# A routed mixture of experts in one core's kernel: another way to the top four, two wide places for four, and token selection turned round

## The chip, the cores and the metric

The kernel runs on one core of one Trainium2 chip. The metric is device time in microseconds for one execution; the median of three runs stands for the kernel.

## The reference

Three transformer blocks are applied to 256 tokens of width 1024, in fp32. The change lies in the first block's mixture of experts (32 experts, top 4, inner width 1024):

```python
logits = h @ w_router + b_router
top_v, top_i = lax.top_k(logits, 4)
gates = softmax(top_v)
# for each expert e, for the tokens xb that chose it:
u = xb @ w_mlp1[e] + b_mlp1[e]                      # 1024 -> 2048
x_glu = minimum(u[..., ::2], 7.0)
x_lin = clip(u[..., 1::2], -7.0, 7.0)
a = x_glu * sigmoid(1.702 * x_glu) * (x_lin + 1)
y = a @ w_mlp2[e] + b_mlp2[e]                       # 1024 -> 1024
# out[token] += gate * y
```

256 tokens and 4 choices make 1024 assignments, 32 an expert on average. The weights of an expert are 12 MiB, those of all 384 MiB.

## The kernel before

The program is written out by hand for five engines: a function `X_pe`, `X_act`, `X_dve` or `X_sp` holds what TensorE, ScalarE, VectorE or the loading queue (SyncE) does in stage X, in program order. Engines meet over counters: `then_inc(*k.DVE("perm"))` counts up and marks, `wait_ge(*k.dve("perm"))` waits. The eight PSUM banks are handed out by `k.bank` in rotation, and the next user of a bank waits until it has been read out. "Place" is the word for a position p = 0..31 in the order in which experts are worked on; "group" is a set of up to 64 or 128 slots for tokens in it.

**Router** (`route_pe`, `route_act`, `route_dve`). x lies with its 1024 features in eight chunks of 128 partitions (`x[:, c, :]`, 256 tokens wide). 16 matmuls (L1592) make the logits, tokens on partitions, 32 columns. `to_tok_pe` (L714) transposes x to token rows, `htok`. VectorE finds the four largest of 32 by counting for every logit how many stand above it: comparisons of all pairs, 1024 elements a partition, ties to the lower index (L1647 to L1660), and a mask of those with fewer than four above (L1663). Matmuls with a triangle of ones (L1598 to L1604) count each token's position within its expert and the experts' totals. From these VectorE makes `posm` (position or -1), the matrix `perm` that sorts experts by their totals (L1687), the gates, and on place 0 the selection matrix `P` (tokens x slots, a one where a token takes a slot).

**Order of the places.** Place 0 is always expert 0, so its weights can be loaded before the router is done. The other 31 experts are sorted by how many tokens chose them, and `RANKS` says which rank comes to which place. The places in `WIDE` get the largest ones and two groups (128 slots); all others have one group of `CAP = 64` slots. So there are 32 + len(WIDE) groups, and `OF[p]` lists those of place p. If any expert has more tokens than its place has slots, `count` is positive and `overflow_*` runs all experts again on a slow path.

**Experts** (`experts_pe`, from L1881). For each place p, TensorE goes through 8 up steps, c = 0..7, one for each chunk of `w_mlp1` (`up_pe`, L1781): for each group four matmuls with 64 stationary columns of `xg` (the selected tokens, features on partitions) and 512 moving columns of weights, in two column tiles (h = 0, 1) that run side by side. Between the steps stand other pieces: after c = 1 the transposes of the previous place's activation (`turn_a_pe`, L1828), after c = 3 the scatter of the place before that (L1868), after c = 5 the selection of the next place's tokens (`select_x_pe`, L1744) and the transposes of its gated selection matrix (`select_g_pe`, L1752). Then come the bias (L1792) and the previous place's 4 down steps (L1851). `select_x_pe` holds 16 matmuls a group:

```python
for d in range(KC):
    for b in range(2):
        m = e.matmul(bank[:, d * CAP:(d + 1) * CAP], t["htok"][:, b, d * 128:(d + 1) * 128], t[f"P{n % 3}"][:, b, :], start=b == 0, stop=b == 1)
```

**Weights** (`experts_sp`, L1959). Each load is 1 MiB and goes to one of `NEXP = 9` slots. Load m waits until load m - 9 has been used. Loads 0 to 7 (place 0's up) go out before the router is done; load 8 waits for `idx`, the sorted list of experts. A place has 8 up loads and 4 down loads, the latter behind the next place's up loads.

Of the kernel before, what the change touches and what calls it, by code (L numbers as in the profile page):

```python
# [16 lines left out]
KC = 8  # L17
# [5 lines left out]
WIDE = (0, 8, 16, 24)  # L23
# [8 lines left out]

RANKS = [NE - 1 if p == 0 else WIDE.index(p) - 1 if p in WIDE else p - 1 + sum(1 for w in WIDE[1:] if w > p) for p in range(NE)]

EARLY = ("tri", "swa1", "iota", "ids", "idcol", "keyrow", "keycol", "ranks", "r64", "r128", "r256", "b32", "pick2")


def const_arrays():  # L40
# [9 lines left out]
    c["pick2"] = ((i % 32 == 0) & (j < 64) | (i % 32 == 16) & (j >= 64)).astype(f32)  # L50
    c["tri"] = (i < j).astype(f32)
# [54 lines left out]
class Mute:  # L106
# [7 lines left out]
    copy_predicated = memset = dma_start = bn_stats = bn_aggr = If = nothing  # L114
# [1470 lines left out]
def route_pe(k, e):  # L1585
    t = k.t
    e.wait_ge(*k.act("pre2", "out", 3))
    e.wait_ge(*k.dve("pre2", "out", 7))
    bank = k.bank(e, "logits")
    for b in range(2):  # L1590
        for c in range(KC):
            m = e.matmul(bank[:, b * NE:(b + 1) * NE], t["x"][:, c, b * 128:(b + 1) * 128], t["wr"][:, c, :], start=c == 0, stop=c == KC - 1)  # L1592
# [16 lines left out]
    e.wait_ge(*k.dve("perm"))  # L1609
    perm = t["perm"][0:NE, :]  # L1610
    e.matmul(k.bank(e, "idx")[0:1, 0:NE], k.cc("idcol")[0:NE, :], perm).then_inc(*k.MM("idx"))
    bank = k.bank(e, "gT")
    e.wait_ge(*k.dve("gates"))
    for b in range(2):
        e.transpose(bank[0:NE, b * 128:(b + 1) * 128], t["gates"][:, b, :], k.cc("ident"))
        m = e.transpose(bank[0:NE, 256 + b * 128:256 + (b + 1) * 128], t["posm"][:, b, :], k.cc("ident"))
    m.then_inc(*k.MM("gT"))
    bank = k.bank(e, "perm")
    e.wait_ge(*k.act("gT"))
    for i in range(4):  # L1620
# [22 lines left out]
def route_dve(k, e):  # L1643
    t = k.t
    L, mask, gates, st = t["L"], t["mask2"][:, :, 0:NE], t["gates"], t["st"]
    ids = k.cc("ids")
    e.tensor_tensor(t["etri"], over(ids, NE), along(ids, NE), ALU.is_lt).then_inc(*k.DVE())  # L1647
# [3 lines left out]
    for b in range(2):  # L1651
        other, own = L[:, b:b + 1, :].to_broadcast([128, NE, NE]), along(L[:, b, :], NE)
        e.tensor_tensor(t["cmp0"], other, own, ALU.is_equal).then_inc(*k.DVE())
        e.wait_ge(*k.dve())
        e.tensor_tensor(t["cmp0"], t["cmp0"], t["etri"], MUL).then_inc(*k.DVE())
        e.tensor_tensor(t["cmp1"], other, own, ALU.is_gt).then_inc(*k.DVE())
        e.wait_ge(*k.dve())
        e.tensor_tensor(t["cmp0"], t["cmp0"], t["cmp1"], ADD).then_inc(*k.DVE())
        e.wait_ge(*k.dve())
        e.tensor_reduce(t["above"][:, b, :], t["cmp0"], AX.X, ADD).then_inc(*k.DVE())  # L1660
        e.wait_ge(*k.dve())
    for i in range(2):
        e.tensor_scalar(t["mask2"][:, :, i * NE:(i + 1) * NE], t["above"], 3.5, None, ALU.is_lt).then_inc(*(k.DVE("mask") if i else k.DVE()))  # L1663
# [2073 lines left out]
```

## Time and profile before

| | |
|---|---|
| median of 3 runs | 2960.89 us (2958.17 to 2964.32) |
| profiled execution, its own time | 2964.16 us |
| its span | 2962.3 us |
| mean granted TensorE clock | 0.953 |
| TensorE busy | 2793.4 us, 94% |
| VectorE, ScalarE busy | 47%, 31% |
| bytes moved | 713.75 MB, of them 384 loads of 1 MiB of expert weights |

The span runs from the first to the last instruction. Three stretches follow one another without overlap on TensorE: what lies before the router (0 to 235 us), router and experts (235 to 1311 us), and the two other blocks (to 2962 us).

### The profile page before, as it was taken

What the parts mean: (1) busy time and instruction counts of PE and PEld (TensorE: products, weight loads), DVE (VectorE), ACT (ScalarE), POOL (GpSimd) and SP (SyncE); (2) the same over time, 40 slices, a digit from 0 to 9 for tenths busy, and PEclk for the clock granted to TensorE, in tenths of its full rate; (3) what the DMA queues carried; (4) which work ended last, traced back from release to release, by engine and by line L of the source; (5) the groups of instructions that cost most, each with busy time, mean ns of one, the idle gap of its engine ahead of it and who ended that gap; (6) DMA issues with size and microseconds to landing.
All of it is one profiled execution on the core that took longest, in us unless ns stands there. A gap on an engine that the chain in (4) does not pass through costs nothing. (4 is left out here: it accounts for less than half of the span.)

```text
span 2962.3 us, 41639 instructions
## 1 busy us (share of the span) xinstructions
PE 2793.4 (94%) x17530; PEld 2006.9 (68%) x17530; DVE 1394.8 (47%) x1995; ACT 925.6 (31%) x1220; POOL 223.5 (8%) x160
## 2 busy tenths in 40 slices
PE   7887999999999999977899989999999999999998
PEld 5655344443443433426879979989889989898897
DVE  3553222222122222227767765576575575665655
ACT  4342010111011100024455543345343443425433
POOL 1100000000000000000000010027020020102200
PEclk8975999999999999987799989999999999999999
DMA  8633899999999999974235555555556546440453
GB/s 292 210 121 144 314 399 417 372 381 417 415 353 402 416 371 380 417 295 131 72 128 191 195 165 195 190 167 175 171 183 203 181 166 205 147 160 30 157 199 114
DMA packets 292711, 713.75 MB, mean 241 GB/s; under 512 B 15587, under 2 KB 189369, under 8 KB 259430
## 3 DMA queue, kind: packets, MB, share of 16 engines
q1 hardware_dynamic: 281168, 690.27, 63.1%
q10 hardware_dynamic: 9734, 17.02, 1.8%
q0 software_dynamic: 1616, 3.72, 0.4%
q8 instruction: 141, 2.31, 0.3%
q14 instruction: 52, 0.43, 0.0%
HBM read 709.91 MB, written 1.05 MB: 240 GB/s over the span
## 5 line engine op out<-in xcount | busy, mean ns | idle before, releaser
L368 DVE TENSOR_TENSOR lo<-ring,hi 128x2048 fp32r<-128x2048 f32 x251 | 601.0, 2399 | 307.3 <-ACT hi L359 307.3
L359 ACT ACTIVATE hi<-ring 128x2048 fp32r<-128x2048 f32 x251 | 475.5, 1897 | 152.3 <-PE bank L637 125.7
L1781 PE MATMUL bank<-expert,xg 128*64 128x512 f32 x2304 | 522.1, 598 | 0.0
L429 PE MATMUL bank<-x_hi,hi 128*128 128x256 f32 x1568 | 382.8, 284 | 0.0
L429 PE MATMUL bank<-x_lo,hi 128*128 128x256 f32 x1568 | 380.3, 281 | 0.0
L1781 PEld LDWEIGHTS bank<-expert,xg 128*64 128x64 f32 x2304 | 157.4, 137 | 311.0 <-issue 309.8
L429 PEld LDWEIGHTS bank<-x_lo,hi 128*128 128x128 f32 x1568 | 295.6, 189 | 2.5 <-issue 1.0
L429 PEld LDWEIGHTS bank<-x_hi,hi 128*128 128x128 f32 x1568 | 295.0, 188 | 3.3 <-issue 1.6
L1878 DVE TENSOR_TENSOR acc<-bank,acc 128x512 f32<-128x512 f32 x144 | 89.4, 683 | 407.9 <-PE bank L1868 407.7
L1851 PE MATMUL bank<-expert,aT 128*64 128x512 f32 x1152 | 254.9, 595 | 1.2 <-DMA expert<-in_w_mlp 1.2
L1806 DVE TENSOR_SCALAR sx<-bank 128x256 f32<-128x256 f32 x72 | 30.2, 419 | 393.8 <-PE bank L1792 393.3
L434 PE MATMUL bank<-x_hi,lo 128*128 128x256 f32 x1568 | 204.0, 282 | 0.0
L1851 PEld LDWEIGHTS bank<-expert,aT 128*64 128x64 f32 x1152 | 79.6, 137 | 174.2 <-issue 169.8
L434 PEld LDWEIGHTS bank<-x_hi,lo 128*128 128x128 f32 x1568 | 194.8, 188 | 0.0
L1760 ACT ACTIVATE xg<-bank 128x512 f32<-128x512 f32 x36 | 21.5, 597 | 442.7 <-PE bank L1744 442.7
L1744 PEld LDWEIGHTS bank<-P,htok 128*128 128x128 f32 x1152 | 137.8, 200 | 26.3 <-issue 26.3
L637 PE MATMUL bank<-hi,act_hi 128*128 128x512 f32 x448 | 144.5, 396 | 0.0
L637 PE MATMUL bank<-hi,act_lo 128*128 128x512 f32 x448 | 144.4, 396 | 0.0
L1744 PE MATMUL bank<-P,htok 128*128 128x64 f32 x1152 | 142.3, 284 | 1.1 <-DVE P L1675 1.1
L637 PE MATMUL bank<-lo,act_hi 128*128 128x512 f32 x448 | 119.6, 396 | 0.0
L389 ACT ACTIVATE act_hi<-tmp 128x512 fp32r<-128x512 f32 x56 | 35.4, 633 | 253.3 <-DVE tmp L2814 188.7
L637 PEld LDWEIGHTS bank<-lo,act_hi 128*128 128x128 f32 x448 | 84.3, 188 | 20.6
(621 smaller groups left out, 3833.2 us busy)
## 6 DMA issues: line engine op xcount, KB each, us to landing
expert<-in_w_mlp SPq DMA_DIRECT2D x384, 1024.0 KB, 11.6
ring<-in_l_ffn_w_in SPq DMA_DIRECT2D x88, 1024.0 KB, 5.1
ring<-in_l_ffn_w_out SPq DMA_DIRECT2D x44, 1024.0 KB, 4.8
ring<-in_w_ada SPq DMA_DIRECT2D x24, 1024.0 KB, 6.7
ring<-in_l_gm_w_in SPq DMA_DIRECT2D x24, 1024.0 KB, 5.1
ring<-in_ffn_w_up SPq DMA_DIRECT2D x22, 1024.0 KB, 5.1
ring<-in_w_in SPq DMA_DIRECT2D x21, 1024.0 KB, 5.7
ring<-in_l_gm_w_out SPq DMA_DIRECT2D x12, 1024.0 KB, 4.8
```

The costliest lines, as they stand in the source:

```text
L359: e.activation(k.half("hi", u), k.slot(j), ACT.Copy).then_inc(*k.up("hi_done"))
L368: e.tensor_tensor(k.half("lo", u), k.slot(k.units[u][0]), k.half("hi", u).bitcast(F32), SUB).then_inc(*k.up("lo_done"))
L389: e.activation(hi[:, c:n, :], x[:, c:n, :], ACT.Copy).then_inc(*k.ACT(nm, "hi", c // step))
L429: e.matmul(o, l, r, start=fresh, stop=False, skip_group_check=True)
L434: t = e.matmul(o, l, r, start=False, stop=False, skip_group_check=True)
L637: m = e.matmul(acc[b, h][:, :], x[:, c, b * 128:(b + 1) * 128], w[:, c, h * 512:(h + 1) * 512], start=fresh[b, h], stop=False, skip_group_ ...
L1744: m = e.matmul(bank[:, d * CAP:(d + 1) * CAP], t["htok"][:, b, d * 128:(d + 1) * 128], t[f"P{n % 3}"][:, b, :], start=b == 0, stop=b == 1)
L1760: e.activation(flat(k.t[f"xg{n % 3}"]), k.got("xg", n)[:, :], ACT.Copy).then_inc(*k.ACT("xg", n, frees=("xg", n)))
L1781: i = e.matmul(banks[n][j][h * CAP:(h + 1) * CAP, :], x, W[:, (2 * h + j) * 512:(2 * h + j + 1) * 512], start=c == 0, stop=False, skip_gro ...
L1806: e.tensor_scalar(t[f"sx{j}"], bank[:, 0:512:2], 7.0, None, MIN).then_inc(*k.DVE("gate", "x", n, j))
L1851: q = e.matmul(banks[n][h * CAP:(h + 1) * CAP, :], a, W[:, r, h * 512:(h + 1) * 512], start=i + r == 0, stop=i + r == 4, skip_group_check= ...
L1878: e.tensor_tensor(av, k.got("back", n, b, h)[:, :], av, ADD).then_inc(*k.DVE(frees=("back", n, b, h)))
```

## The change

**Logits.** The roles of x and the router's weights are exchanged: weights (32 columns) are stationary, 256 tokens move. Chunk c goes to column tile c % 4, so that four partial sums stand at partitions 0, 32, 64 and 96 of one bank. ScalarE copies them to `parts`, and two matmuls with `fold` (a constant, four stacked 32x32 identities) add the four and turn the result to tokens on partitions. Each chunk is waited for by itself.

**Top four.** `max` gives the eight largest of a token's 32 logits, `max_index` their positions. The first four positions are compared with 0..31 and summed to the mask.

**Places.** `WIDE` is (8, 20); place 0 has one group of 64 slots. There are 34 groups, not 36.

**Selection.** P (64 slots) becomes stationary and `htok` moves with 512 columns: four matmuls in two column tiles, result with slots on partitions. ScalarE copies it to `xs`, four transposes turn it (`turn_x_pe`), ScalarE copies to `xg`. Selection stands after c = 4 and the turn after c = 6.

**Moved.** The transposes of gates and positions, their permutation, and the product with `b_mlp2` no longer stand ahead of place 0 but inside it, after c = 0, 1 and 3 (`route_rest_pe`); the G transposes of place 0 after its c = 4. The index list comes ahead of the gates' last steps.

```diff
-WIDE = (0, 8, 16, 24)
+WIDE = (8, 20)
...
+    c["fold"] = (i % 32 == j[:, 0:32]).astype(f32)
...
 def route_pe(k, e):
     t = k.t
-    e.wait_ge(*k.act("pre2", "out", 3))
-    e.wait_ge(*k.dve("pre2", "out", 7))
+    bank = k.bank(e, "logits4")
+    for c in range(KC):
+        if c < 4:
+            e.wait_ge(*k.act("pre2", "out", c))
+        else:
+            e.wait_ge(*k.dve("pre2", "out", c))
+        q = 32 * (c % 4)
+        m = e.matmul(bank[q:q + 32, 0:256], t["wr"][:, c, :], t["x"][:, c, :], start=c < 4, stop=c >= 4, skip_group_check=True)
+    m.then_inc(*k.MM("logits4"))
     bank = k.bank(e, "logits")
+    e.wait_ge(*k.act("logits4"))
     for b in range(2):
-        for c in range(KC):
-            m = e.matmul(bank[:, b * NE:(b + 1) * NE], t["x"][:, c, b * 128:(b + 1) * 128], t["wr"][:, c, :], start=c == 0, stop=c == KC - 1)
+        m = e.matmul(bank[:, b * NE:(b + 1) * NE], t["parts"][:, b * 128:(b + 1) * 128], k.cc("fold"))
...
     for n in OF[0]:
         select_x_pe(k, e, n)
     e.wait_ge(*k.dve("perm"))
+    e.matmul(k.bank(e, "idx")[0:1, 0:NE], k.cc("idcol")[0:NE, :], t["perm"][0:NE, :]).then_inc(*k.MM("idx"))
+    for n in OF[0]:
+        turn_x_pe(k, e, n)
+
+
+def route_rest_pe(k, e, c):
...
     for b in range(2):
-        other, own = L[:, b:b + 1, :].to_broadcast([128, NE, NE]), along(L[:, b, :], NE)
-        e.tensor_tensor(t["cmp0"], other, own, ALU.is_equal).then_inc(*k.DVE())
-        e.wait_ge(*k.dve())
-        e.tensor_tensor(t["cmp0"], t["cmp0"], t["etri"], MUL).then_inc(*k.DVE())
-        e.tensor_tensor(t["cmp1"], other, own, ALU.is_gt).then_inc(*k.DVE())
-        e.wait_ge(*k.dve())
-        e.tensor_tensor(t["cmp0"], t["cmp0"], t["cmp1"], ADD).then_inc(*k.DVE())
-        e.wait_ge(*k.dve())
-        e.tensor_reduce(t["above"][:, b, :], t["cmp0"], AX.X, ADD).then_inc(*k.DVE())
-        e.wait_ge(*k.dve())
+        e.max(t["best"][:, b, :], L[:, b, :]).then_inc(*k.DVE())
+    e.wait_ge(*k.dve())
+
+    for b in range(2):
+        e.max_index(t["which"][:, b, :], t["best"][:, b, :], L[:, b, :]).then_inc(*k.DVE())
+    e.tensor_tensor(gates, L, t["best"][:, :, 0:1].to_broadcast([128, 2, NE]), SUB).then_inc(*k.DVE("gates", "less"))
+    e.wait_ge(*k.dve())
+    e.tensor_copy(t["whichf"], t["which"]).then_inc(*k.DVE())
+    e.wait_ge(*k.dve())
+    for b in range(2):
+        e.tensor_tensor(t["hits"][:, b, :, :], along(t["whichf"][:, b, 0:4], NE), over(k.cc("ids"), 4), ALU.is_equal).then_inc(*k.DVE())
+    e.wait_ge(*k.dve())
     for i in range(2):
-        e.tensor_scalar(t["mask2"][:, :, i * NE:(i + 1) * NE], t["above"], 3.5, None, ALU.is_lt).then_inc(*(k.DVE("mask") if i else k.DVE()))
+        e.tensor_reduce(t["mask2"][:, :, i * NE:(i + 1) * NE], t["hits"].rearrange("p b j e -> p b e j"), AX.X, ADD).then_inc(*(k.DVE("mask") if i else k.DVE()))
...
 def select_x_pe(k, e, n):
+
     t = k.t
+    bank = k.bank(e, "xs", n)
+    e.wait_ge(*k.dve("P", n))
+    for b in range(2):
+        for h in range(2):
+            m = e.matmul(bank[h * CAP:(h + 1) * CAP, :], t[f"P{n % 3}"][:, b, :], t["htok"][:, b, h * 512:(h + 1) * 512], start=b == 0, stop=b == 1, skip_group_check=True)
+    m.then_inc(*k.MM("xs", n))
+
+
+def turn_x_pe(k, e, n):
+
     bank = k.bank(e, "xg", n)
-    e.wait_ge(*k.dve("P", n))
-    for d in range(KC):
-        for b in range(2):
-            m = e.matmul(bank[:, d * CAP:(d + 1) * CAP], t["htok"][:, b, d * 128:(d + 1) * 128], t[f"P{n % 3}"][:, b, :], start=b == 0, stop=b == 1)
+    e.wait_ge(*k.act("xs", n))
+    for i in range(4):
+        m = e.transpose(bank[:, i * 128:(i + 1) * 128], k.t[f"xs{n % 2}"][:, i * 128:(i + 1) * 128], k.cc("ident"))
     m.then_inc(*k.MM("xg", n))
...
 def experts_pe(k, e):
-    for n in OF[0]:
-        select_g_pe(k, e, n)
     for p in range(NE + 1):
         if p < NE:
             ups = {n: [k.bank(e, "up", n, j, hold=True) for j in range(2)] for n in OF[p]}
         for c in range(KC):
             if p < NE:
                 up_pe(k, e, p, c, ups)
+            if p == 0:
+                route_rest_pe(k, e, c)
...
-            elif c == 5 and p + 1 < NE:
+            elif c == 4 and p + 1 < NE:
                 for n in OF[p + 1]:
                     select_x_pe(k, e, n)
+                for n in OF[p + 1] + (OF[0] if p == 0 else []):
                     select_g_pe(k, e, n)
+            elif c == 6 and p + 1 < NE:
+                for n in OF[p + 1]:
+                    turn_x_pe(k, e, n)
```

TensorE from the selection for place 0's second group (`P_89`; that of the first stands ahead of it) to the first up matmuls (L1781, `expert`) before; L1611 is the index list, L1615 to L1622 gates, positions and capacities in the order of the places, L1625 the product with `b_mlp2`, L1752 the G transposes:

```order
L1744 MATMUL bank<-P_89,htok 128x64 x16
L1611 MATMUL bank<-perm,early 1x32
L1615 MATMUL bank<-const,gates 32x128
L1616 MATMUL bank<-const,posm 32x128
L1615 MATMUL bank<-const,gates 32x128
L1616 MATMUL bank<-const,posm 32x128
L1621 MATMUL bank<-perm,gT 128x32 x4
L1622 MATMUL bank<-caps,one_19 128x32
L1625 MATMUL bank<-b_30,gT 128x512 x4
L1752 MATMUL bank<-const,Pg_86 128x128 x2
L1752 MATMUL bank<-const,Pg_90 128x128 x2
L1781 MATMUL bank<-expert,xg_88 64x512 x4
```

The same stretch of the change; L1765 is the selection, L1774 the turn, L1818 the up matmuls, L1632 to L1642 and L1646 what stood at L1615 to L1625:

```order
L1765 MATMUL bank<-htok,P_84 64x512 x4
L1619 MATMUL bank<-perm,early 1x32
L1774 MATMUL bank<-const,unit 128x128 x4
L1818 MATMUL bank<-expert,xg_87 64x512 x4
L1632 MATMUL bank<-const,gates 32x128 x2
L1634 MATMUL bank<-const,posm 32x128 x2
L1818 MATMUL bank<-expert,xg_87 64x512 x4
L1641 MATMUL bank<-perm,gT 128x32 x4
L1642 MATMUL bank<-caps,one_19 128x32
L1818 MATMUL bank<-expert,xg_87 64x512 x8
L1646 MATMUL bank<-b_30,gT 128x512 x4
L1818 MATMUL bank<-expert,xg_87 64x512 x4
```

Up matmuls begin behind the turn, and the rest of the router's work stands between them. A narrow place in the steady run before, from its first up step to its down steps (L1851):

```order
L1781 MATMUL bank<-expert,xg_92 64x512 x8
L1828 MATMUL bank<-const,share 128x128 x4
L1781 MATMUL bank<-expert,xg_92 64x512 x8
L1868 MATMUL bank<-share,G_99 128x512 x4
L1781 MATMUL bank<-expert,xg_92 64x512 x8
L1744 MATMUL bank<-P_93,htok 128x64 x16
L1752 MATMUL bank<-const,Pg_94 128x128 x2
L1781 MATMUL bank<-expert,xg_92 64x512 x8
L1792 MATMUL bank<-b_32,perm 64x512 x4
L1851 MATMUL bank<-expert,aT_87 64x512 x16
```

Selection and G transposes stand together there, between the sixth and the seventh step. In the change (L1865 activation's transposes, L1905 scatter, L1829 bias, L1888 down):

```order
L1818 MATMUL bank<-expert,xg_95 64x512 x8
L1865 MATMUL bank<-const,share 128x128 x4
L1818 MATMUL bank<-expert,xg_95 64x512 x8
L1905 MATMUL bank<-share,G_99 128x512 x4
L1818 MATMUL bank<-expert,xg_95 64x512 x4
L1765 MATMUL bank<-htok,P_84 64x512 x4
L1782 MATMUL bank<-const,Pg_85 128x128 x2
L1818 MATMUL bank<-expert,xg_95 64x512 x8
L1774 MATMUL bank<-const,unit 128x128 x4
L1818 MATMUL bank<-expert,xg_95 64x512 x4
L1829 MATMUL bank<-b_32,perm 64x512 x4
L1888 MATMUL bank<-expert,aT_90 64x512 x16
```

16 selection matmuls of 64 columns behind the sixth up step have become 4 of 512 behind the fifth, and 4 transposes stand behind the seventh.

## Rows read from the trace of the kernel before

**Rows 1.** Windows: stretch, busy us of each engine (instructions), granted clock, DMA share, GB/s
```profile
235.00:285.00 50.00, 38.09 (x156) 32.00 (x157) 19.80 (x50) 8.46 (x15) 0.00 (x0) 0.53 0.20 77
285.00:1311.00 1026.00, 1021.44 (x5332) 413.49 (x5330) 221.87 (x565) 102.00 (x213) 0.00 (x0) 1.00 0.97 386
```
**Rows 2.** Waits of the loading queue, 220 to 1290 us: total, times, longest
```profile
SPq L1975 <- PE bank L1781: 416.3, 155, 16.0
```
**Rows 3.** Timeline of TensorE, one narrow place: start us, us, what
```profile
1242.94 3.60 PE L1781 MATMUL bank<-expert,xg 128*64 128x512 f32 x16
1246.47 0.66 PE L1828 MATMUL bank<-const,share 128*128 128x128 f32 x4
...
1256.15 3.79 PE L1744 MATMUL bank<-P,htok 128*128 128x64 f32 x32
1259.77 0.39 PE L1752 MATMUL bank<-const,Pg 128*128 128x128 f32 x2
...
1271.61 3.60 PE L1781 MATMUL bank<-expert,xg 128*64 128x512 f32 x16
```
**Rows 4.** Windows within the first loads and the experts
```profile
226.00:228.00 2.00, 0.00 (x0) 0.00 (x0) 0.32 (x2) 1.34 (x4) 0.00 (x0) 0.50 1.02 430
...
400.00:540.00 140.00, 140.00 (x756) 59.68 (x756) 29.65 (x80) 14.76 (x31) 0.00 (x0) 1.00 1.02 417
560.00:580.00 20.00, 20.00 (x108) 7.33 (x109) 6.71 (x20) 3.13 (x7) 0.00 (x0) 1.00 0.72 263
```
**Rows 5.** Timeline of TensorE, last place and end of the experts
```profile
1281.23 7.09 PE L1781 MATMUL bank<-expert,xg 128*64 128x512 f32 x32
1288.25 1.09 PE L1792 MATMUL bank<-b,perm 32*64 32x512 f32 x8
...
1295.70 1.94 PE L1851 MATMUL bank<-expert,aT 128*64 128x512 f32 x8 [0.60 <-DMA expert<-in_w_mlp]
...
1305.99 1.94 PE L1851 MATMUL bank<-expert,aT 128*64 128x512 f32 x8 [0.31 <-DMA expert<-in_w_mlp]
1308.69 1.99 PE L1868 MATMUL bank<-share,G 64*128 64x512 f32 x8 [0.76 <-ACT share L1859]
```
**Rows 6.** Timeline of all engines, router to first up matmul
```profile
234.73 7.01 PE L1592 MATMUL bank<-wr,x 128*128 128x32 f32 x32 [1.61 <-ACT x L489]
...
241.54 3.22 PE L714 MATMUL bank<-const,x 128*128 128x128 f32 x16
241.77 0.22 DVE L1649 TENSOR_TENSOR L<-bank,br 128x64 f32<-128x64 f32 x1 [6.01 <-PE bank L1592]
...
243.53 0.60 ACT L722 ACTIVATE htok<-bank 128x512 f32<-128x512 f32 x1 [0.26 <-PE bank L714]
...
254.58 0.21 DVE L1664 TENSOR_REDUCE st<-L 128x2 f32<-128x64 f32 x1
...
254.81 0.61 PE L1598 MATMUL bank<-mask,early 128*128 128x32 f32 x2 [10.05 <-DVE st L1664]
...
258.73 13.89 PE L1744 MATMUL bank<-P,htok 128*128 128x64 f32 x64 [1.09 <-DVE P L1675]
...
276.67 7.17 PE L1625 MATMUL bank<-b,gT 32*128 32x512 f32 x8
...
284.81 22.66 PE L1781 MATMUL bank<-expert,xg 128*64 128x512 f32 x96
```
**Rows 7.** Timeline of TensorE in the first stage: four column tiles of 32
```profile
8.20 1.94 PE L1077 MATMUL bank<-ring,sc 128*32 128x512 f32 x8 [0.67 <-DVE sc L729]
```
**Rows 8.** Loading queue: load 8 in its timeline; issue to landing of line L1975
```profile
274.00 0.36 SPq L1975 DMA_DIRECT2D expert<-in_w_mlp  x1
...
DMA to landing us min/median/max: 4.7/11.0/19.9
```
**Rows 9.** Windows: first block, TensorE waiting for weights; and after the first up matmuls
```profile
120.00:130.00 10.00, 5.63 (x46) 2.14 (x44) 3.46 (x10) 2.46 (x5) 0.00 (x0) 1.00 1.05 394
...
288.00:290.00 2.00, 2.00 (x10) 0.66 (x8) 0.00 (x0) 0.00 (x0) 0.00 (x0) 0.86 0.00 0
```

More of the change, by code:

```diff
@@ L29 @@
 NEXP = 9
-RANKS = [NE - 1 if p == 0 else WIDE.index(p) - 1 if p in WIDE else p - 1 + sum(1 for w in WIDE[1:] if w > p) for p in range(NE)]
-EARLY = ("tri", "swa1", "iota", "ids", "idcol", "keyrow", "keycol", "ranks", "r64", "r128", "r256", "b32", "pick2")
+RANKS = [NE - 1 if p == 0 else WIDE.index(p) if p in WIDE else p - 1 + sum(1 for w in WIDE if w > p) for p in range(NE)]
+EARLY = ("tri", "swa1", "iota", "ids", "idcol", "keyrow", "keycol", "ranks", "r64", "r128", "r256", "b32", "pick2", "fold")
 def const_arrays():
@@ L1634, in route_act @@
         select_x_act(k, e, n)
+    for n in OF[0]:
+        turn_x_act(k, e, n)
     e.wait_ge(*k.mm("gT"))
@@ L1645, in route_dve @@
     L, mask, gates, st = t["L"], t["mask2"][:, :, 0:NE], t["gates"], t["st"]
-    ids = k.cc("ids")
-    e.tensor_tensor(t["etri"], over(ids, NE), along(ids, NE), ALU.is_lt).then_inc(*k.DVE())
     e.wait_ge(*k.mm("logits"))
@@ L1756, in select_x_act, with turn_x_act @@
 def select_x_act(k, e, n):
+    if n >= 2:
+        e.wait_ge(*k.mm("xg", n - 2))
+    e.wait_ge(*k.mm("xs", n))
+    e.activation(k.t[f"xs{n % 2}"], k.got("xs", n)[:, :], ACT.Copy).then_inc(*k.ACT("xs", n, frees=("xs", n)))
+def turn_x_act(k, e, n):
     if n >= 3:
@@ L1777, in up_pe @@
     for n in OF[p]:
-        x = t[f"xg{n % 3}"][:, c, :]
+        x = t[f"xg{n % 3}"][:, 2 * (c % 4) + c // 4, :]
         for j in range(2):
@@ L1917, in experts_act @@
 def experts_act(k, e):
-    for n in OF[0]:
-        select_g_act(k, e, n)
     for p in range(NE + 1):
@@ L1926, in experts_act @@
                 select_x_act(k, e, n)
+            for n in OF[p + 1] + (OF[0] if p == 0 else []):
                 select_g_act(k, e, n)
+            for n in OF[p + 1]:
+                turn_x_act(k, e, n)
         if p < NE:
@@ L2110, in lay_moe @@
         bi("mask2", 128, 2, 2 * NE)
-        for n in ("L", "above", "gates", "posm", "gov", "gatp", "posp"):
+        for n in ("L", "gates", "posm", "gov", "gatp", "posp"):
             bi(n, 128, 2, NE)
@@ L2118, in lay_moe @@
             bi(f"xg{i}", 128, KC, CAP)
+        for i in range(2):
+            k.t[f"xs{i}"] = flat(k.t["unit"])[:, i * 512:(i + 1) * 512]
+        bi("best", 128, 2, 8), bi("whichf", 128, 2, 8), k.sb("which", [128, 2, 8], mybir.dt.uint32, ci)
         for i in range(5):
@@ L2124, in lay_moe @@
         share = bi("share", 128, 3072)
-        for i, n in enumerate(("cmp0", "cmp1", "etri")):
-            k.t[n] = share[:, i * 1024:(i + 1) * 1024].rearrange("p (a b) -> p a b", a=NE)
+        k.t["parts"] = share[:, 0:256]
+        k.t["hits"] = share[:, 256:512].rearrange("p (b j e) -> p b j e", b=2, j=4)
         for i in range(3):
```

62 lines of the change are left out of this document (32 added, 30 removed).

## The prediction

> **What bounds the kernel now.** I read the windows by stage first, to find which stretch the change touches and what is full there. The router stretch, 235 to 285 us, has TensorE at a granted clock of 0.53 and DMA at 0.20 [rows 1]: neither the array nor the weight stream works at its rate, so this is a chain of dependent steps. The expert stretch, 285 to 1311 us, has TensorE busy for 1021.4 of 1026 us at clock 1.00 and DMA at 0.97 [rows 1]: two resources are nearly full, and it must be settled which one sets the pace.
>
> The waits of the loading queue come next. It waited 416.3 us in total for up matmuls to free a slot [rows 2], so TensorE sets the pace now. Its own timeline shows the period of a place with one group: the first up run of one place starts at 1242.94, that of the next at 1271.61 [rows 3], 28.67 us. A place needs 12 loads of 1 MiB. Where the stream never rests it moves 417 GB/s [rows 4], 2.515 us a load, 30.2 us a place. So a narrow place is *shorter* than its weights' transfer, and only four wide places let the nine slots fill again: DMA falls to 263 GB/s around one of them [rows 4]. At the end the lead is used up: TensorE waits for weights at 1295.70 and 1305.99 [rows 5]. This is the point on which the forecast turns: TensorE work taken away below 30.2 us a place is not gained in full.
>
> **The router to the first up matmul: 50.1 us now (234.73 to 284.81) [rows 6].**
> - Logits. Now 16 matmuls at half clock, 234.73 to 241.54, then VectorE starts at 241.77. New: four column tiles of 32, two rounds of 256 columns. The nearest row is one round of four tiles with 512 columns at half clock, 1.94 us [rows 7], so 0.97 each. The first round can start before the last chunks of x are there; I put the end at 235.7. ScalarE's copy of 256 columns takes under the 0.60 of a 512-column one [rows 6]: 0.4, plus 0.1 to be woken. Two matmuls at (241.54 - 234.73)/16 = 0.43 make 0.9. VectorE starts at 237.2, 4.6 us earlier.
> - The mask. Now 254.81 - 241.77 = 13.0 us. New: one add, two MAX, two MAX_INDEX, one subtraction, one cast, two comparisons and two reductions, all on at most 256 elements a partition. MAX and MAX_INDEX are in no row. Bound below by a reduction over 64 elements, 0.21 us [rows 6]; above by an eleventh of the old 13.0 us, 1.2 each. I take 0.2, since they read 32 elements, and for the wider ones 0.3 to 0.4: 2.8 us, mask at 240.1. At 1.2 each it would be 4 us more. The transposes of x to token rows (16 in 3.2 us, behind the logits on TensorE) end at 240.4 and become the later of the two.
> - Places and P: the same as now, 254.81 to 258.73, 3.9 us: P at 244.2.
> - Selection for place 0: now 13.9 us, two groups at half clock [rows 6]. New: one group, four column-tiled matmuls with 512 moving columns. At half clock two rounds, twice 1.71 = 3.4: 247.8. Copy 0.7, turn (4 transposes at 0.2) 0.9, copy 0.8: first up matmul at 250.3.
> - What stood behind it (gate transposes, permuted gates, the b2 product, the G transposes, 272.6 to 284.8) now lies inside place 0. It still costs TensorE time there.
>
> So the first up matmul comes **34.5 us earlier**. The expert index is copied at about 248.5, and load 8, issued at 274.00 now [rows 8], goes out at 249.
>
> **A narrow place.** A run of 16 up records lasts 1246.47 - 1242.94 = 3.53 to 3.59, one of 32 lasts 1288.25 - 1281.23 = 7.02 [rows 3, 5]. So 8 records (four column-tiled calls) cost 1.71 and each start of a run 0.17. Selection takes 1259.77 - 1256.15 = 3.62 now [rows 3]. New: 1.71 for the four calls, which continue an up run, 0.60 for four transposes (0.66 with the drain) [rows 3], and 0.17 because the up run is cut once more: 2.48. **The period falls from 28.67 to 27.5 us**, 2.8 below the transfer's 30.3. The copy to xs is hidden by the two up steps between selection and turn (3.4 us against 0.6); should it come late it would hold TensorE, but ScalarE is idle nine tenths of the time.
>
> A rule is to be weighed here. The row gives 0.15 us for each transpose. The Trainium skill (TensorE: Matmul & The Clock Gate, Part 4) states some 275 ns for a PE transpose in a kernel and that its time is the array's SBUF latency, which would make four of them 1.1 us. The period would be 28.0 and the end some 5 us later; the trace of four transposes in 0.60 us does not agree, and I go by it.
>
> **Two wide places instead of four.** Each narrow group taken out saves TensorE one group's work, some 26.5 us (28.67 less the run starts that it shares). But it also takes away the time in which the slots refill.
>
> **The sum goes by the stream.** Place 0 needs about 23 us at full clock: 8 x 1.71, one selection 2.5, bias 1.0, and 5.7 of moved steps (the b2 product 3.4, half of what it takes at half clock now [rows 6], the rest small matmuls). The clock rises some 4 us after the first up matmul now, 0.86 in 288 to 290 [rows 9]: with that and the small steps between I take 8 us at half clock, so 27: its last chunk is free at 276. Its load lands 4.7 later, the shortest time from issue to landing [rows 8]: 280.7. From there 367 loads follow. The stretches without rest give 417 GB/s [rows 4], but the last four loads landed in 1305.99 - 1295.70 = 10.3 us [rows 5], 2.57 each. I take 2.525: 926.7 us, to 1207.4. The stream rests when a wide place gives TensorE too much work: a wide place owes 26.5 - 2.8 us more than the transfer, the nine slots can take up 9 x 2.525 - 4.7 = 18.0, so it rests 5.7, twice 11.4: 1218.8. From the last wait to the last matmul's end 4.7 us [rows 5]: **1223.5 against 1310.7 now**. The gain is 87. By TensorE's work alone it would be 34.5 for the start, 18 for place 0's second group (less what was moved into it), 26.5 for the other group and 33 x 1.2 for the selections, 118: some 30 us of it turns into waits for weights, in the places before the second wide one and in the last ones.
>
> The profiled execution took 2964.2 us (span 2962.3), 3.3 over the median of 2960.9. 2964.2 - 87.2 = 2877.0; at the median level **2874 us**. What follows the experts is unchanged and starts from the same meeting point.
>
> **Rivals.**
> 1. *The stream runs faster once it never rests.* For: 430 GB/s in 2 us of the first loads, with little else going on [rows 4]. Against: 140 us without rest at 417, at a share of 1.02 [rows 4]. At 2.467 us a load the end comes 376 x 0.058 = 22 us earlier, less 6 us in which the stream then rests more: 2858. The Trainium skill (DMA: Bandwidth & Descriptors, § Where 436 GB/s comes from) has near 425 GB/s for large transfers on one core, which is that price; the trace's 417 doesn't agree. 14%.
> 2. *Late start and cold clock.* MAX costs 1.2, or small matmuls in place 0 hold the clock at 1.2 GHz through all of it (it stayed at half through the 13.9 us of selection now, though the engine was busy). 4 to 7 us for the first, up to 13 for the second; with loads at 2.55 another 9 less. Time about 2892. Later falls of the clock in the waits for weights would need to cost over 2.8 us a place to show at all, since TensorE has that to spare; a stretch in which it was busy 5.6 of 10 us beside a full stream kept 1.00 [rows 9]. 18%.
> 3. *Slower: overflow.* Places other than the two wide ones take 64 tokens. If the third largest expert, or expert 0, has more than 64, the counter is positive and the slow path runs over all 32 experts without any overlap: 32 x 12 loads x 2.52 = 968 us of transfers alone, and 128 up and 32 down matmuls an expert of 256 and 512 columns in full width (a round of 512 takes 1.71 / 2 = 0.85 us, so 0.43 and 0.85) add 82 us an expert, 2,620 in all: to about 6,500. Routing the reference's drawn inputs gives 68, 63 and 62 as the largest counts and 28 for expert 0, so two tokens are to spare; from the third more in one expert on it decides. 3%.
> 4. *The narrower place does not pay*, because the stream was the only bound already: against it stand the 416 us that the queue waited for TensorE [rows 2]. Then only the earlier start is left: 2961 - 34 = 2927. 3%.
>
> **The numbers.** The forecast case has 62%, rival 1 14%, rival 2 18%, the rest as given. Within the first, the load price (2.50 to 2.55: -7 to +7) and the start (4 us either way) give 2862 to 2886. The range reaches to the first two rivals: 2852 to 2900. A measurement can tell 0.2%, 6 us. Faster by more: all but overflow and an unforeseen stall, 0.95; within: 0.01; slower: 0.04.
>
> **What would show it.** First up matmul at 250 us, not 285. Narrow places of 27.5 us after each wide one and of 30.2 before the second wide one and at the end; DMA share 1.02 nearly throughout and the loading queue's wait for TensorE shorter, while TensorE's idle time before up and down matmuls, released by the expert tile's DMA, comes to 25 to 35 us. Experts end at about 1223. It is wrong if the weights' waits stay under 10 us, if the first up matmul comes after 258, or if a saturated load takes other than 2.49 to 2.56 us.

## The result, and the profile after

| | before | after |
|---|---|---|
| median | 2962.6 us (4 runs) | 2878.0 us (2875.8 to 2884.7, 4 runs) |
| ratio, 95% interval | | 0.972 (0.9699 to 0.9741) |
| profiled execution, span | 2964.2, 2962.3 us | 2879.2, 2877.4 us |
| last x chunk written (VectorE) | 234.6 | 239.0 |
| first up matmul | 284.8 | 253.4 |
| end of the last scatter matmul | 1310.7 | 1234.0 |
| that end less the last x chunk, "the stretch" | 1076.1 | 995.0 |
| TensorE's waits for expert weights | 1.2 | 25.6 |
| from there to the end | 1651.6 | 1643.4 |

The change is 2.8% faster. The first block ended 4.4 us later in the profiled run and the rest was 8.2 us shorter, though neither is touched; over the profiles of the table below the end of the first block lies between 233.9 and 239.0 and the rest between 1643 and 1654 us. So the stretch from the last x chunk to the last scatter is the measure in what follows. It fell by 81.1 us; 87.2 had been forecast. The totals differ by 84.6 us, so some 3.5 us of that come from stretches that the change does not touch.

The windows of the kernel after, with the columns of [rows 1]: the whole of the steady stream, two stretches without rest and the two around the wide places.

```profile
285.00:1229.00 944.00, 918.23 (x4290) 293.08 (x4288) 205.36 (x523) 113.81 (x229) 0.00 (x0) 1.00 1.01 410
...
500.00:600.00 100.00, 100.00 (x480) 33.25 (x478) 24.24 (x60) 12.30 (x25) 0.00 (x0) 1.00 0.98 388
600.00:860.00 260.00, 250.26 (x1166) 78.87 (x1162) 54.65 (x144) 32.24 (x65) 0.00 (x0) 1.00 1.02 417
880.00:960.00 80.00, 80.00 (x388) 26.64 (x386) 21.71 (x56) 10.83 (x22) 0.00 (x0) 1.00 0.97 375
960.00:1220.00 260.00, 248.56 (x1148) 76.97 (x1146) 54.62 (x136) 29.37 (x59) 0.00 (x0) 1.00 1.02 417
```

TensorE, which was busy for 1021.4 of 1026 us [rows 1], is now idle for 944.0 - 918.2 = 25.8 us, and the DMA share has gone from 0.97 to 1.01. Away from the wide places the stream moves 417 GB/s without a pause. The waits (total, times, longest); first TensorE's, then the loading queue's, for first-layer loads (L2017) and second-layer loads (L2024):

```profile
PE bank L1818 <- DMA expert<-in_w_mlp: 22.4, 39, 1.6
PE bank L1888 <- DMA expert<-in_w_mlp: 3.2, 8, 0.6
```

```profile
SPq L2017 <- PE bank L1818: 278.5, 129, 6.5
SPq L2024 <- PE bank L1818: 166.5, 94, 3.6
SPq L2017 <- PE bank L1888: 157.3, 90, 4.1
SPq L2024 <- PE bank L1888: 44.4, 30, 2.9
```

The line that stood at 416.3 us before [rows 2] is 278.5, and TensorE waits for weights 47 times. But the queue's four waits for matmuls still add to 646.7 us (787.7 before), although the stream runs full away from the wide places: while the queue waits for one slot, eight other loads may be landing or lie ready. Its waits alone do not tell who sets the pace; the GB/s of the windows do. The router, in the timeline of all engines:

```profile
237.46 2.73 PE L1596 MATMUL bank<-x,wr 128*32 128x256 f32 x16
...
240.22 0.38 ACT L1652 ACTIVATE share<-bank 128x256 f32<-128x256 f32 x1 [2.00 <-PE bank L1596]
...
240.75 1.03 PE L1601 MATMUL bank<-early,share 128*128 128x32 f32 x4 [0.57 <-ACT share L1652]
...
241.82 0.22 DVE L1672 TENSOR_TENSOR L<-bank,br 128x64 f32<-128x64 f32 x1 [2.78 <-PE bank L1601]
242.08 0.29 DVE L1675 MAX8 best<-L 128x8 f32<-128x32 f32 x2
242.40 0.09 DVE L1679 MATCH_VALUE_LOAD which<-best,L 128x8 f32 x1
242.48 0.18 DVE L1679 FIND_INDEX8 which<-best,L 128x8 uint32<-128x32 f32 x1
...
243.72 1.11 DVE L1688 TENSOR_REDUCE mask<-share 128x64 f32<-128x256 f32 x2
...
245.04 0.36 PE L1607 MATMUL bank<-mask,early 128*128 128x32 f32 x2
...
247.71 2.95 PE L1765 MATMUL bank<-htok,P 128*64 128x512 f32 x8 [1.09 <-DVE cnt L1702]
...
253.42 2.83 PE L1818 MATMUL bank<-expert,xg 128*64 128x512 f32 x6 [0.89 <-ACT xg L1797]
```

Eight logit matmuls take 2.73 us, the fold 1.03, and VectorE starts 2.8 us after the last x chunk (7.2 before). Two MAX take 0.29, a MAX_INDEX is a load of 0.09 and a search of 0.18; mask and start of the position matmuls are at 245.04, 3.2 us later, against 13.0 [rows 6]. Selection for place 0 takes 2.95 instead of 13.89. Then a narrow place while the lead lasts, and the last place, in TensorE's timeline:

```profile
615.28 3.60 PE L1818 MATMUL bank<-expert,xg 128*64 128x512 f32 x16
618.82 0.66 PE L1865 MATMUL bank<-const,share 128*128 128x128 f32 x4
...
624.90 1.94 PE L1818 MATMUL bank<-expert,xg 128*64 128x512 f32 x8
626.67 1.89 PE L1765 MATMUL bank<-htok,P 128*64 128x512 f32 x8
628.49 0.44 PE L1782 MATMUL bank<-const,Pg 128*128 128x128 f32 x2
...
632.44 0.66 PE L1774 MATMUL bank<-const,unit 128*128 128x128 f32 x4
...
642.83 3.60 PE L1818 MATMUL bank<-expert,xg 128*64 128x512 f32 x16
```

```profile
1216.60 1.94 PE L1888 MATMUL bank<-expert,aT 128*64 128x512 f32 x8 [0.62 <-DMA expert<-in_w_mlp]
1219.16 1.94 PE L1888 MATMUL bank<-expert,aT 128*64 128x512 f32 x8 [0.62 <-DMA expert<-in_w_mlp]
...
1223.78 5.37 PE L1888 MATMUL bank<-expert,aT 128*64 128x512 f32 x24
1229.34 1.94 PE L1888 MATMUL bank<-expert,aT 128*64 128x512 f32 x8 [0.19 <-DMA expert<-in_w_mlp]
1232.04 1.99 PE L1905 MATMUL bank<-share,G 64*128 64x512 f32 x8 [0.76 <-ACT share L1896]
```

642.83 - 615.28 = 27.55 us is the period, 28.67 before [rows 3]; selection and turn (1.82 and 0.59 from start to start) stand where 3.62 stood. At the end every load is waited for: 2.56 us from 1216.60 to 1219.16 for a step that takes 1.9.

### The profile page after: what moved, and what is told of

It reads as the page before. It is cut to its first block and busy times, and to the rows that moved or that the text cites. A ratio compares the mean times of both kernels' runs of the same rounds, so it can differ in the third digit from the quotient of the medians.

```text
span 2877.4 us, 39681 instructions
## 1 busy us (share of the span) xinstructions
PE 2691.2 (94%) x16538; PEld 1868.0 (65%) x16538; DVE 1366.8 (48%) x1958; ACT 941.1 (33%) x1243; POOL 223.4 (8%) x160
## 5 line engine op out<-in xcount | busy, mean ns | idle before, releaser
L1818 PE MATMUL bank<-expert,xg 128*64 128x512 f32 x2176 | 510.8, 603 | 23.4 <-DMA expert<-in_w_mlp 22.4
L1818 PEld LDWEIGHTS bank<-expert,xg 128*64 128x64 f32 x2176 | 142.9, 137 | 315.0 <-issue 269.6
L1888 PE MATMUL bank<-expert,aT 128*64 128x512 f32 x1088 | 244.1, 597 | 3.3 <-DMA expert<-in_w_mlp 3.2
L1888 PEld LDWEIGHTS bank<-expert,aT 128*64 128x64 f32 x1088 | 73.8, 137 | 171.4 <-issue 149.5
L1790 ACT ACTIVATE unit<-bank 128x512 f32<-128x512 f32 x34 | 20.3, 597 | 287.8 <-PE bank L1765 287.8
L639 PEld LDWEIGHTS bank<-hi,act_lo 128*128 128x128 f32 x448 | 84.3, 188 | 20.6
```

Source lines behind the costliest of these rows:

```text
L639: m = e.matmul(acc[b, h][:, :], x[:, c, b * 128:(b + 1) * 128], w[:, c, h * 512:(h + 1) * 512], start=fresh[b, h], stop=False, skip_group_ ...
L1818: i = e.matmul(banks[n][j][h * CAP:(h + 1) * CAP, :], x, W[:, (2 * h + j) * 512:(2 * h + j + 1) * 512], start=c == 0, stop=False, skip_gro ...
L1888: q = e.matmul(banks[n][h * CAP:(h + 1) * CAP, :], a, W[:, r, h * 512:(h + 1) * 512], start=i + r == 0, stop=i + r == 4, skip_group_check= ...
```

## The experiments

Each place's duration is the distance of the first up runs of two places in TensorE's timeline. Two theories were set against each other. *Stream theory*: a place costs the larger of TensorE's work and its 12 loads (30.2 us), and nine slots carry a limited lead from one to the other. *Work theory*: TensorE's work alone counts, and the waits for weights are incidental.

| kernel | stretch | waits for weights | total |
|---|---|---|---|
| before | 1076.1 | 1.2 | 2962.6 |
| router and moved work only | 1059.5 | 0.8 | 2940.4 |
| selection only | 1043.8 | 10.3 | 2929.4 |
| places only | 1027.7 | 9.0 | 2917.1 |
| change, four wide places | 1021.2 | 9.8 | 2909.3 |
| change, old selection | 1007.7 | 8.2 | 2895.9 |
| change, old top four | 1003.2 | 25.2 | 2893.2 |
| change, eight slots | 1001.2 | 31.7 | 2887.4 |
| change, rest ahead of place 0 | 997.1 | 26.1 | 2883.8 |
| **the change** | 995.0 | 25.6 | 2878.0 |
| one wide place | 983.9 | 37.1 | 2870.0 |
| one wide place, b2 later | 984.4 | 36.6 | 2872.2 |
| change, halved second-layer loads | 956.1 | 0 | 2845.4 |

Totals of kernels other than before, the change and the two with one wide place are single runs, and each stretch and its waits come from one profile. In the change's own profile places 0 and 1 took 53.7 us, with eight slots and with one wide place 50.9 and 51.0, with the same steps in them: TensorE's clock stayed low longer (last section). So differences of 3 us between stretches say nothing.

**The change with four wide places.**

```diff
-WIDE = (8, 20)
+WIDE = (0, 8, 16, 24)
```

> The change with four wide places (0, 8, 16, 24) again; the new router and the new selection stay. Measured as the stretch from the last x chunk's write to the end of the last scatter matmul: 995.0 us in the change, 1076.1 in the kernel before. Stream theory (loads of 2.515 us and nine slots set the pace wherever TensorE needs under 30.2 us a place): 1027, since the two groups put back cost 4 us ahead of place 0, and of their other 44 us of TensorE work some 16 only take the place of waits for weights; those waits fall from 26 to under 13 us. Work theory (TensorE's work is what counts, the waits for weights are incidental): all 48 us come back, 1043.

1021.2, 6 below the stream theory's 1027 and 22 below the work theory's 1043. The seven places between two wide ones took 34.9, 29.3, 27.5, 27.5, 27.5, 29.3 and 31.5. The first two still hold down steps and scatter of the wide place, so up to the fifth TensorE goes at its own pace; in the sixth the lead is gone.

**The change with the old selection.**

```diff
             elif c == 4 and p + 1 < NE:
                 for n in OF[p + 1]:
-                    select_x_pe(k, e, n)
...
+            elif c == 5 and p + 1 < NE:
+                for n in OF[p + 1]:
+                    select_x_pe(k, e, n)
...
-            elif c == 6 and p + 1 < NE:
-                for n in OF[p + 1]:
-                    turn_x_pe(k, e, n)
```

> The change with the old selection: 16 matmuls of 64 columns a group behind the sixth up step, straight to feature rows, no turn. Two wide places and the new router stay. A narrow place needs 28.7 us of TensorE again, not 27.5. Stream theory: that is still below the 30.2 us of a place's loads, so of 4 us at the start and 33 x 1.16 = 38 us in the places about 18 show in all: 1013, waits for weights 8 to 12 us. Work theory: 1037.

1007.7, 5 below the stream theory's 1013. Narrow places took 28.7, so 33 selections put back 1.12 us each, and the first up matmul came 1.3 us later, where 4 had been expected: of 38 us of TensorE work, 12.7 show. 17.4 us of it took the place of recorded waits for weights (25.6 against 8.2), and there were 18 such waits, not 47; with the 0.22 us that each costs beyond its record (see the halved loads) that is 6.4 more. Under 2 us are left.

**One wide place.**

```diff
-WIDE = (8, 20)
+WIDE = (14,)
```

> The change with one wide place (14) in place of two; the largest expert takes it (68 tokens), the next two have 63 and 62 and fit 64 slots. Stream theory: TensorE's work falls by a group, 26.5 us, but only the rest that the stream takes around one wide place (7 to 8 us) is gained: stretch 987, waits for weights 44 to 50 us instead of 26, total about 8 us below the change. Work theory: 26 us below, 969.

983.9, 11.1 below the change; the total is 2870.0 (2869.0 to 2875.8), ratio 0.9694 to before (0.9675 to 0.9714), whose interval overlaps the change's. By the totals it is 7.9 below; up to 2.7 of the 11.1 belong to the clock in places 0 and 1 of the change's profile. TensorE has 26.5 us less to do, and its waits rise by 11.5:

```profile
PE bank L1818 <- DMA expert<-in_w_mlp: 32.6, 60, 0.7
PE bank L1888 <- DMA expert<-in_w_mlp: 4.5, 9, 0.7
```

It has the lowest median of the kernels that compute the reference's function, and it leans on the drawn data: two experts have 63 and 62 tokens for 64 slots.

**Halved loads.** Of each second-layer load only the first half is fetched; the output is of other weights.

```diff
-                e.dma_start(two(k.expert_slot(m)), W[:, 2 * i:2 * i + 2, :])
+                e.dma_start(two(k.expert_slot(m))[:, 0:1, :], W[:, 2 * i:2 * i + 1, :])
```

> The change with every second-layer load halved: only the first of its two 128-row pieces is fetched, the other half of the slot keeps what was there before, so the products with it are of other weights. A place then moves 10 MiB, 25.1 us, less than TensorE's 27.5. Stream theory: the waits for weights vanish almost wholly and the stretch falls by their 26 us, to 969, perhaps to 965; narrow places take 27.5 us everywhere. If something other than the stream held TensorE at 30.2 us a place (the order of the steps, buffer waits), these places would stay at 30.

956.1, below what was expected. The places away from the wide ones took 27.5 to 27.6 us from place 2 on, and in the window TensorE is busy throughout:

```profile
285.00:1190.00 905.00, 904.07 (x4282) 296.47 (x4280) 204.95 (x520) 113.76 (x229) 0.00 (x0) 1.00 0.92 353
```

So nothing but the stream held it back. The 38.9 us are more than the 25.6 of recorded waits. The missing 13 us stand in the change's TensorE-busy time: it is 918.2 us from 285 to 1229, against 904.1 here for the same work. A step that a wait cuts off is shown with 1.94 us (2.56 from start to start less the 0.62 waited, in the last place above), while in an unbroken run 8 more matmuls take 1.72 (8 before a selection 1.77 from start to start, 16 before it 3.49). So each wait costs 0.22 us beyond its record: 47 of them are 10.3 of the 13.3, and 3 stay open. Against before, TensorE's work alone is worth 120 us, as the prediction had reckoned (118); the change gets 81 of them.

**The parts of the change alone, on the kernel before.** First two wide places, with `RANKS` and the capacities to match:

```diff
-WIDE = (0, 8, 16, 24)
+WIDE = (8, 20)
```

> The kernel before with two wide places (8, 20) in place of four, nothing else. Stretch from the last x chunk to the last scatter, 1076.1 before. TensorE's work falls by 7 us at half clock in the selection ahead of place 0, some 27 us for place 0's second group and 26.5 for another. Work theory: 1016. Stream theory: narrow places at 28.7 use up the slots' lead of some 16 us at 1.5 us a place, ten places at most, and each wide place lets the stream rest: 1027, waits for weights about 8 to 10 us.

1027.7, the stream theory's number; the work theory is off by 12. Then the new selection and turn, with the wide places of before:

```diff
+    for b in range(2):
+        for h in range(2):
+            m = e.matmul(bank[h * CAP:(h + 1) * CAP, :], t[f"P{n % 3}"][:, b, :], t["htok"][:, b, h * 512:(h + 1) * 512], start=b == 0, stop=b == 1, skip_group_check=True)
...
+def turn_x_pe(k, e, n):
...
-    for d in range(KC):
-        for b in range(2):
-            m = e.matmul(bank[:, d * CAP:(d + 1) * CAP], t["htok"][:, b, d * 128:(d + 1) * 128], t[f"P{n % 3}"][:, b, :], start=b == 0, stop=b == 1)
```

> The kernel before with the new selection and turn alone; four wide places, old router, nothing moved. TensorE's work falls by 5 to 6 us ahead of place 0 and by 1.16 us for each of 35 groups, 41 us. Work theory: 1029 for the stretch, from 1076.1. Stream theory: 1040 to 1044, with 8 to 13 us of waits for weights at the ends of the runs of seven narrow places, which take 27.5 us until the lead is gone.

1043.8, again the stream theory's. Then the change with both undone (router, mask and the order of the rest stay as changed):

```diff
-WIDE = (8, 20)
+WIDE = (0, 8, 16, 24)
...
-    for n in OF[0]:
-        turn_x_pe(k, e, n)
```

> The change with both the old four wide places and the old selection: what is left is the new router (packed logits, MAX) and the work moved into place 0. P for place 0 was ready 8.4 us after the last x chunk in the change, 24.1 before; with two groups selected the old way at half clock the first up matmul should come 23 to 25 us after it (50.2 before, 14.4 in the change). 5.7 us of moved work lie in place 0. Narrow places take 28.7 us, so both theories say nearly the same: 1076 - 26 + 6 = 1056 to 1060, waits for weights under 4 us. It is needed for the sum of the parts: places alone gave 48.4 us, selection alone 32.3. Stream theory: with 16 to 20 us here they add to about 98, some 17 more than the 81.1 of the whole change. Work theory: they add to 81, and this part gives nothing.

1059.5, 16.6 us. The parts alone add to 48.4 + 32.3 + 16.6 = 97.3, together they give 81.1: 16 us of overlap, as the stream theory had it. The same part is worth less the more of the others is there: two places for four give 48.4 us to the kernel before and 26.2 to the change, the new selection 32.3 and 12.7.

**Eight slots.**

```diff
-NEXP = 9
+NEXP = 8
```

> The change with eight slots for weights, not nine. Stream theory: the lead that TensorE can live on falls by one load, 2.5 us, so the stream rests 2.5 us longer at each wide place and the narrow places reach 30.2 us one place earlier: 1002 for the stretch (995.0 with nine), waits for weights 6 to 8 us more. Work theory, or a stream that always has enough queued: 995.

1001.2, 6.2 us more, waits 6.1 more. With one load less of lead the places from the third behind the first wide one on took 27.5, 27.5, 29.1, 30.1, where nine slots gave 27.5, 27.5, 27.5, 28.8, 30.1. Since the change's profile had the slower start, the price may be up to 2.8 us more.

**The old top four.**

```diff
     for b in range(2):
-        e.max(t["best"][:, b, :], L[:, b, :]).then_inc(*k.DVE())
+        other, own = L[:, b:b + 1, :].to_broadcast([128, NE, NE]), along(L[:, b, :], NE)
+        e.tensor_tensor(t["cmp0"], other, own, ALU.is_equal).then_inc(*k.DVE())
...
```

> The change with the old way to the four largest (all pairs compared) in place of MAX and MAX_INDEX; packed logits stay. The mask took 3.0 us of VectorE time from the logits in the change, 13.0 before: the first up matmul comes 10 us later (24.4 after the last x chunk, not 14.4), and since nothing of the weight stream beyond load 7 can go out before the index list, the stretch grows by the same 10, to 1005. If the stream could catch up a late start, it would stay near 995 to 1000.

First up matmul 25.6 us after the last x chunk, 11.2 later than in the change, but the stretch grew by 8.2 only: places 0 and 1 took 49.5 us, 53.7 in the change's profile. Some 2.7 us of that difference belong to the clock in the change's own profile.

**The rest ahead of place 0 again.**

```diff
         turn_x_pe(k, e, n)
+    for c in range(4):
+        route_rest_pe(k, e, c)
...
-            if p == 0:
-                route_rest_pe(k, e, c)
```

> The change with the transposes of gates and positions, their permutation and the b2 product ahead of place 0 again, at half clock, some 11 us. First up matmul 25 us after the last x chunk, not 14.4; place 0 shorter by 5.7 us, or a little less. The index list and load 8 go out as in the change, but loads 9 to 16 wait for place 0's steps. Stream theory: 5 to 6 us more, 1000 to 1001. If these steps were fully on the path: 1006. If the stream had something to do meanwhile: 995.

997.1, below the 1000 to 1001 of the stream theory: up matmuls 9.6 us later, the stretch 2.1 longer. The b2 product took 7.17 us ahead of place 0 and 3.70 within, but places 0 and 1 were 8.5 us shorter. 2.1 us is less than the places 0 and 1 of two profiles may differ by here, so the gain of this move is small, and whether it is above zero stays open.

**The b2 product one place later**, on the kernel with one wide place.

```diff
-            elif c == 3 and p >= 2:
+            elif c == 3 and p == 1:
+                b2_pe(k, e)
+            elif c == 3 and p >= 2:
```

> The kernel with one wide place, and the product with b_mlp2 (four matmuls, 3.6 us) moved on from place 0 to place 1, behind its fourth up step, where no scatter stands. TensorE's work is the same. Stream theory: place 0's last four chunks come free 3.6 us earlier, so the stream is in step that much earlier, and the 3.6 us in place 1 are taken from waits for weights later on: stretch 980 against 983.9, total 2 to 4 us below the kernel with one wide place (2870.0). Work theory: no change, 984.

984.4 and 2872.2 (2864.6 to 2877.9): no gain; my expectation was wrong. Place 0 did become shorter (21.5 us, 25.4 with one wide place alone), but place 1 took 31.0 instead of 25.5, 2 us more than the product's 3.6, and at places 0 and 1 TensorE's work still sets the pace: the slots fill up, and what the stream gains by an earlier start it rests later on. The windows show both, the clock and the rest of the stream (columns as in [rows 1]):

```profile
280.00:284.00 4.00, 4.00 (x13) 1.55 (x10) 0.00 (x0) 1.33 (x3) 0.00 (x0) 1.00 1.03 419
286.00:288.00 2.00, 2.00 (x8) 0.55 (x6) 0.00 (x0) 0.00 (x0) 0.00 (x0) 0.50 1.06 434
290.00:294.00 4.00, 4.00 (x19) 1.31 (x20) 0.00 (x0) 0.87 (x2) 0.00 (x0) 1.00 0.68 244
```

**No wide place.**

```diff
-WIDE = (8, 20)
+WIDE = ()
```

> The change with no wide place at all. The largest expert has 68 tokens and its place 64 slots, so the counter is positive and the slow path runs over all 32 experts. This prices the prediction's overflow rival: 968 us of transfers without overlap and 2,620 us of matmuls, about 3,590 us more than the change's 2878, less 14 us for the stream's rest at two wide places: 6,450. Bounds: 968 us more if the matmuls lay under the transfers, and up to 4,500 more if every bank's readout is waited for.

7452.8 us, 4,575 more than the change. The path is real and its price was taken 1,000 us too low: the granted clock is 0.86 there, and every load is waited for. The windows of experts and slow path, and two waits in it:

```profile
240.00:1180.00 940.00, 889.48 (x4063) 275.84 (x4061) 194.13 (x515) 114.99 (x228) 0.00 (x0) 0.99 1.00 409
1180.00:5830.00 4650.00, 3085.63 (x10404) 2198.88 (x10405) 655.46 (x1710) 123.52 (x293) 4.72 (x5) 0.86 0.26 90
```

```profile
PE bank L2064 <- DMA expert<-in_w_mlp: 1044.7, 128, 9.6
...
PE bank L2075 <- DMA expert<-in_w_mlp: 501.2, 64, 8.6
```

The matmuls keep TensorE busy for 3,086 us, 96 an expert and not 82, and the waits for weights are 1,546 us, where I had the transfers' bare 968.

## Why the prediction held, point by point

- **The start.** Forecast 34.5 us earlier at the first up matmul, measured 50.2 - 14.4 = 35.8 after the last x chunk. VectorE started 2.8 us after it (2.6 forecast), the mask took 3.2 (2.8 and the wait for the transposes), selection at half clock 3.0 (3.4).
- **What sets the pace.** The mechanism held, but one reading of it did not carry the weight put on it: "It waited 416.3 us ... so TensorE sets the pace now". In the change the queue waits 646.7 us beside a full stream. What did carry it is the comparison of 28.67 with 30.2 us and the fall to 263 GB/s at the wide places [rows 3, 4].
- **The narrow place.** 27.5 forecast, 27.5 measured. Its parts were forecast as 1.71 for the selection, 0.60 for the turn and 0.17 for one more cut of the up run. They came out as 1.82, 0.59 and 0.09: from 3.62 to 2.41 for the first two is 1.21, and the period fell by 1.12.
- **Place 0.** 27 us forecast, with one stretch of half clock; its period was 28.15, and its last chunk came free 41.6 us after the last x chunk, against 41.4 forecast. That match is partly luck: the start was 1.3 us better, and the clock rose a little later and fell a second time inside the place, which was not forecast. Where it did not, with eight slots or one wide place, the period was 25.4.
- **The stream's start.** "Its load lands 4.7 later" was right for one load by itself only. Place 0 frees its slots unevenly: four steps in the last 9 us, where loads take 2.5 us each. Before that the stream had nearly stood still, as the window at 270 to 275 shows. Eight loads had landed by 248, when the stream stood, and the queue moved 8.70 MB, 8.3 loads, from 252 to 285 (packets, MB, share of 16 engines). So 16.3 had moved by 285.0, 46.0 us after the last x chunk, where 17 were counted: **1.7 us** late, start and place 0 included.

```profile
248.00:250.00 2.00, 2.00 (x8) 0.48 (x4) 1.01 (x6) 0.00 (x0) 0.00 (x0) 0.62 0.00 0
270.00:275.00 5.00, 5.00 (x21) 1.64 (x19) 0.42 (x2) 0.95 (x3) 0.00 (x0) 0.76 0.36 110
```

```profile
q1 hardware_dynamic: 1228, 8.70, 73.1%
```

- **The stream's rest at the wide places** was forecast as 5.7 us each: 23.7 owed less a lead of 18.0. Measured: 100 x (417 - 388) / 417 = 7.0 us and 80 x (417 - 375) / 417 = 8.1, together 15.1, **3.7 more**. Both sizes were too large and largely cancel, which is luck. A wide place's work spreads over its neighbours: the places 7, 8 and 9 took 31.4, 42.1 and 34.9 us, 17.9 more than three places' loads and not 23.7 (18.9 at the second). And the places behind used up 0.9 + 3 x 2.6 + 1.3 = 10 us until one was held up (29.3, three times 27.5, 28.8 against 30.2), so the lead is about 10 and not 18. With eight slots the same sum gives 7.3, one load less.
- **The load price.** 2.525 forecast, 2.515 measured (417 GB/s): 367 x 0.010 = 3.7 less, which cancels the line above.
- **What else was in the stream** had no term in the forecast. From 1225.8 on the last 0.4 load shared the queue with the next stage's loads and took 3.6 us where 1.1 is its price, **2.5 more**. The queues for instructions moved 0.70 MB beside the experts, **1.7 us**.
- **Sum.** +1.7, +3.7, -3.7, +2.5 and +1.7 make 5.9 of the 6.1 us by which the stretch came out longer than forecast; from the last wait to the end it is 4.7 us, as forecast. In the total, 2878.0 against 2874: there the untouched stretches gave back a part of the 6.1, by chance.
- **The waits**: 25.6 us, forecast 25 to 35.
- **The rivals.** The faster stream did not come: 417 GB/s in every stretch without rest, 260 us long twice. The Trainium skill's 425 for a transfer of 16 MB (DMA: Bandwidth & Descriptors, § Measured) was not reached. (The rival's price counts 376 loads where the sum has 367, a slip of 0.5 us.) MAX and MAX_INDEX cost 0.15 and 0.27, so the late start did not come either. Of the cold clock a part came, within place 0; it did not fall in the waits for weights: 1.00 from 285 to 1229. Overflow did not come, and the narrower place did pay: from the parts, selection alone is worth 32.3 us to the kernel before. The Trainium skill's 275 ns for a transpose, given there for bf16 (TensorE: Matmul & The Clock Gate, Part 4), would have given a period of 28.0; here four in fp32 took 0.59 us.

## What to carry to other kernels

When two resources are both near full, take the unit of work (here a place) and compare its price on each: 28.7 us of TensorE against 30.2 of transfers said, before any run, that the first 1.2 us saved per place would be worth little where the lead was used up, and that only the slots' refill at the wide places made TensorE look like the bound. Then savings no longer add: price each part with the others in place. And a prefetch ring hides a mismatch only for as many units as its lead holds. Measure that lead: here it was about 10 us, where nine slots times the load time less one load's flight had given 18.

## What the runs showed of the hardware that was not expected

- **The clock fell under a busy TensorE.** In the kernel with the product in place 1, TensorE was busy without a gap, and yet the clock was 0.50 at 286 to 288 (windows above), right behind it; the next up step and selection took 3.14 and 2.42 us:

```profile
280.99 3.69 PE L1649 MATMUL bank<-b,gT 32*128 32x512 f32 x8
284.62 3.14 PE L1825 MATMUL bank<-expert,xg 128*64 128x512 f32 x8
287.54 2.42 PE L1772 MATMUL bank<-htok,P 128*64 128x512 f32 x8
```

  The change's profile shows the same behind the product in place 0:

```profile
265.02 3.70 PE L1646 MATMUL bank<-b,gT 32*128 32x512 f32 x8
268.65 3.40 PE L1818 MATMUL bank<-expert,xg 128*64 128x512 f32 x8
271.83 2.17 PE L1765 MATMUL bank<-htok,P 128*64 128x512 f32 x8
```

  With one wide place the product stands at the same point, and in its profile the up step behind it took 1.94:

```profile
260.80 3.70 PE L1646 MATMUL bank<-b,gT 32*128 32x512 f32 x8
264.42 1.94 PE L1818 MATMUL bank<-expert,xg 128*64 128x512 f32 x8
```

  From the start of the product's successor to the G transposes that is 5.3 us against 3.6, so 1.7 of the 2.7 us by which places 0 and 1 differ in these two profiles (53.7 and 51.0); the other 1.0 lies in the steps ahead of the product. With halved loads the clock fell at the same point. Why it falls in some executions was not tested. In the kernel before, the clock stayed at 0.50 from 258 to 272 us, while TensorE ran the selection without a gap from 258.73 on [rows 6].
- **A switch of the way the array is tiled costs 0.05 to 0.1 us.** From start to start, 16 up matmuls ahead of transposes took 3.54 us (615.28 to 618.82) and 8 selection matmuls ahead of transposes 1.82 (626.67 to 628.49), so one takes 0.215 and 0.10 is left to each run. Half of that is there without a switch too: 8 up matmuls ahead of the selection, in the same tiling, took 1.77 (624.90 to 626.67). Ahead of the bias 8 took 1.87. The prediction's 0.17 for a start rested on the modelled ends of runs and was too much. The Trainium skill (TensorEngine Tiling, § Key Properties) states that changing the mode drains the array; the rows agree, and put the price at no more than 0.1 us.
- **Less than half of the second wide place's work is gained when it goes**: 26.5 us of work taken out gave 11.1 and left 11.5 us more of recorded waits, and the 22 added ones cost 4.8 us beyond the record at 0.22 each.
